# Two attention mixers of the second block: other places for the projections and for the result blocks among the heads' steps

## The reference

```python
h = rms_norm_2(x, norm_mix[l]) * (1 + sc_a) + sh_a
proj = h @ w_in[l]                                    # 1024 -> 3072 features
mq, mk, mv, dq, dk, dv = jnp.split(proj, splits, axis=-1)     # six parts of 512
mq = apply_partial_rope(rms_norm_2(heads(mq, MOBA_HEADS, HEAD_DIM), moba_q_norm[l]), cos, sin)   # mk, dq, dk alike
o_m = rms_norm_2(moba_attention(mq, mk, mv), moba_out_norm[l])          # 8 heads of 64
o_d = rms_norm_2(diff_attention(dq, dk, dv, lam), diff_subln[l]) * (1.0 - lam_init)   # 4 heads, two score matrices each
x = x + g_a * (jnp.concatenate([o_m, o_d], axis=-1) @ w_out[l])
```

## Time and profile before

| | us |
|---|---|
| median of three runs | 2174.84 (2174.81 to 2177.36) |
| the profiled execution | 2174.54 |
| its span on the engines | 2172.7 |
| layer 0's mixer, first product to last product's end (PE) | 1431.98 to 1601.53 |
| layer 1's mixer | 1811.94 to 1970.07 |

### The profile page before, as it was taken

One profiled execution on the slowest core, in us unless ns is written; L12 is line 12 of the kernel. 1 busy time (PEld: TensorE's weight loads), 2 busy tenths in 40 slices (PEclk: granted clock), 3 DMA queues, 4 the chain that ended last, 5 costly groups with the idle time before them and its releaser, 6 DMA issues.

```text
span 2172.7 us, 28353 instructions
## 1 busy us (share of the span) xinstructions
PE 1996.6 (92%) x11530; PEld 1728.1 (80%) x11530; DVE 1680.0 (77%) x1765; ACT 1174.4 (54%) x1318; POOL 72.8 (3%) x121
## 2 busy tenths in 40 slices
PE   6878999978889999999999999877889999889999
PEld 6666898777568888888788788667779999878998
DVE  6675888877588889899899988888668896846444
ACT  3443333364367776777777677545543445644432
POOL 6001000000100000000000000000010000000000
PEclk7988999998899999999999999978789999968999
DMA  9743799732389999999999999936229995313552
GB/s 350 240 168 136 281 335 366 277 129 97 137 303 330 350 367 355 338 354 371 337 344 363 368 333 352 320 115 223 70 98 345 349 370 163 131 48 128 180 189 97
DMA packets 251209, 554.37 MB, mean 255 GB/s; under 512 B 10077, under 2 KB 75857, under 8 KB 251073
## 3 DMA queue, kind: packets, MB, share of 16 engines
q1 hardware_dynamic: 247252, 544.13, 70.3%
q0 software_dynamic: 3552, 8.29, 1.2%
q10 hardware_dynamic: 268, 0.07, 0.0%
HBM read 551.40 MB, written 1.05 MB: 254 GB/s over the span
## 4 chain that ended last, share of the span: by engine, by line
PE 71%; DVE 14%; ACT 7%; DMA 4%; issue 4%; SPq 0%; ACTq 0%; DVEq 0%
PE bank L497 21%; PE bank L498 21%; PE bank L499 21%; DVE ring_lo L1914 4%; ACT ring_hi L1239 3%; DMA ring<-in_w_in_dram 2%; PE bank L886 1%; DVE acc L1854 1%; DMA ring<-in_ffn_w_dram 1%; PE bank L579 1%; DMA ring<-in_ada_w_dram 1%; PE bank L1064 1%; PE bank L548 1%; DVE XN L2158 1%; DVE work L2096 1%
## 5 line engine op out<-in xcount | busy, mean ns | idle before, releaser
L1914 DVE TENSOR_TENSOR ring_lo<-ring,ring_hi 128x2048 fp32r<-128x2048 f32 x417 | 949.9, 2285 | 267.7 <-ACT ring_hi L1239 265.1
L1239 ACT ACTIVATE ring_hi<-ring 128x2048 fp32r<-128x2048 f32 x417 | 795.5, 1913 | 493.0 <-PE bank L499 239.2
L497 PE MATMUL bank<-hh,ring_hi 128*128 128x256 f32 x1152 | 333.1, 289 | 19.9 <-ACT QK L1433 8.8
L498 PE MATMUL bank<-hl,ring_hi 128*128 128x256 f32 x1152 | 331.0, 287 | 0.0
L499 PE MATMUL bank<-hh,ring_lo 128*128 128x256 f32 x1152 | 330.6, 287 | 0.0
L497 PE MATMUL bank<-ring_hi,hh 128*128 128x256 f32 (+2 forms) x672 | 217.8, 324 | 39.4 <-ACT PT L1383 10.2
L497 PEld LDWEIGHTS bank<-hh,ring_hi 128*128 128x128 f32 x1152 | 226.4, 197 | 24.7 <-issue 14.1
L499 PE MATMUL bank<-ring_hi,hl 128*128 128x256 f32 (+2 forms) x768 | 241.9, 315 | 0.0
L497 PE MATMUL bank<-ring_hi,hgh 128*128 128x512 f32 (+1 forms) x576 | 220.3, 383 | 8.9 <-DVE ring_lo L1914 4.0
L498 PEld LDWEIGHTS bank<-hl,ring_hi 128*128 128x128 f32 x1152 | 226.5, 197 | 0.7 <-issue 0.2
L499 PEld LDWEIGHTS bank<-hh,ring_lo 128*128 128x128 f32 x1152 | 226.3, 196 | 0.0
(11 more groups left out here) (422 smaller groups left out, 2806.1 us busy)
## 6 DMA issues: line engine op xcount, KB each, us to landing
ring<-in_moe_w_dram SPq DMA_DIRECT2D x264, 1024.0 KB, 5.3
ring<-in_ada_w_dram SPq DMA_DIRECT2D x48, 1024.0 KB, 7.2
ring<-in_w_mod_dram SPq DMA_DIRECT2D x48, 1024.0 KB, 7.3
ring<-in_w_in_dram SPq DMA_DIRECT2D x40, 1024.0 KB, 6.4
ring<-in_ffn_w_dram SPq DMA_DIRECT2D x33, 1024.0 KB, 5.7
ring<-in_w_gate_dram SPq DMA_DIRECT2D x22, 1024.0 KB, 5.0
ring<-in_w_up_dram SPq DMA_DIRECT2D x22, 1024.0 KB, 5.1
ring<-in_w_down_dram SPq DMA_DIRECT2D x22, 1024.0 KB, 5.0
```

The costliest lines, as they stand in the source:

```text
L497: pe.matmul(ps, xh, wh, start=first, stop=False)
L498: pe.matmul(ps, xh, wl, start=False, stop=False)
L1239: act.activation(ring_hi[i % NH][:, 0:z], ring[n % NS][:, 0:z], ACT.Copy).then_inc(*s.hi(("hi", home(s, i), i)))
L1914: dve.tensor_tensor(ring_lo[n % NS][:, 0:z], ring[n % NS][:, 0:z], hi, ALU.subtract).then_inc(*s.lo(("lo", home(s, i), i)))
```

## The change

- The list of blocks (`WIN2`) and all three programs take the projections 6, 7, 8, 9, 0, 1 first (before: 6 to 11). So two projections of values (10, 11) leave the front, and 2, 3, 10, 11, 4 lie among the differential heads' steps, 5 among the first steps of the block attention.
- On PE the projections 2, 3, 11, 4 and 5 are cut in two pieces by tile of tokens (24 matmuls each), with a step of the heads between the pieces (2 and 3 share a gap: second piece of 2, first of 3). Projection 10 stays whole.
- Result blocks 2 and 3 are cut in the same way (24 matmuls into 12 and 12): before, block 2 stood whole after step 4 of the block attention and block 3 whole behind all steps. Now they are put as pieces after steps 4, 5 and 7; the second piece of block 3 stands where the whole one stood.
- In `last_blocks` the first tile of tokens now takes all of block 0 before block 1.
- The projections take their banks from `R2`, no longer from `R`.
- ACT and DVE follow the new order. The split of result block 1 moves from behind all heads' work to step 7 (`out_block(3)` on ACT, `block("wout2", 3)` on DVE). The transposes' copies of group 2 come before group 3's squares; the sums of squares and the root of group 0 come ahead of the first head; some splits are ahead of the place of their projection (`halves_for`). A head waits only for the values' block that holds its own columns (`wv`).

The diff, without the lines of `out_block`'s and the heads' dictionaries that only carry the new arguments:

```diff
-        WIN2 = [6, 7, 8, 9, 10, 11, 0, 1, 2, 3, 4, 5]
+        WIN2 = [6, 7, 8, 9, 0, 1, 2, 3, 10, 11, 4, 5]
...
-                    for h in range(2):
-                        for i in blocks:
-                            if t == 0 and h == 0:
-                                pe.wait_ge(*at("y", name, l, i))
-                            wh, wl = weights(main, name, l, i)
-                            for k in range(2):
...
+                    for h, i in ([(h, i) for i in blocks for h in range(2)] if t == 0 else [(h, i) for h in range(2) for i in blocks]):
+                        if t == 0 and h == 0:
+                            pe.wait_ge(*at("y", name, l, i))
+                        wh, wl = weights(main, name, l, i)
...
-                def project(i):
-                    summed(turn_of["win2", l, i])
+                def project(i, tiles=range(2)):
+                    if 0 in tiles:
+                        summed(turn_of["win2", l, i])
+                        psum2(*M, "proj", i)
...
-                    ps = psum(*M, "proj", i)
-                    for t in range(2):
+                    ps = R2.of(*M, "proj", i)
+                    for t in tiles:
...
-                for i in (6, 7, 8, 9, 10):
+                R2.start()
+                for i in (6, 7, 8, 9):
                     project(i)
                 turn_group(2)
-                project(11)
+                project(0)
+                project(1)
                 turn_group(3)
                 diff = attention((*M, "diff"), diff_heads(l))
-                for i in range(4):
-                    next(diff)
-                    project(i)
+                moba = attention((*M, "moba"), moba_heads(l))
                 next(diff)
+                project(2, (0,))
+                next(diff)
+                project(2, (1,))
+                project(3, (0,))
+                next(diff)
+                project(3, (1,))
+                project(10)
                 turn_group(0)
-                project(4)
                 next(diff)
-                project(5)
+                project(11, (0,))
+                next(diff)
+                project(11, (1,))
+                next(diff)
+                project(4, (0,))
                 turn_group(1)
                 next(diff)
-                moba = attention((*M, "moba"), moba_heads(l))
-                next(moba)
-                next(moba)
+                project(4, (1,))
+                next(moba)
+                project(5, (0,))
+                next(moba)
+                project(5, (1,))
                 next(moba)
                 to_features((*M, "yT"), YK, [[(*M, "diff")]] * 2, range(2, 4))
                 next(moba)
                 next(moba)
-                out_block("wout2", l, 2, [], True)
-                for i in range(5, 11):
-                    next(moba)
+                out_block("wout2", l, 2, [("free", *key) for key in R2.held if key], True, (0,))
+                R2.start()
+                next(moba)
+                out_block("wout2", l, 2, [], True, (1,))
+                next(moba)
+                next(moba)
+                out_block("wout2", l, 3, [], False, (0,))
+                next(moba)
+                next(moba)
+                next(moba)
                 to_features((*M, "yT"), YK, [[(*M, "moba", 0)]] * 2, (0,))
-                out_block("wout2", l, 3, [], False)
+                out_block("wout2", l, 3, [], False, (1,))
                 to_features((*M, "yT"), YK, [[(*M, "moba", 1)]] * 2, (1,))
                 last_blocks("wout2", l, 0, 1)
 
...
-                         wv=[(*M, "v", j) for j in range(2)] if h == 0 else []) for h in range(8)]
+                         wv=[(*M, "v", h // 4)] if h % 4 == 0 else []) for h in range(8)]
...
-                         wv=[(*M, "v", j) for j in (2, 3)] if h == 0 else [], lam=lam[:, l:l + 1]) for h in range(4)]
+                         wv=[(*M, "v", 2 + h // 2)] if h % 2 == 0 else [], lam=lam[:, l:l + 1]) for h in range(4)]
...
-                    act.activation(dst, R.of(*M, "proj", i)[:, :].rearrange("p (t c) -> p t c", t=2), ACT.Copy).then_inc(
+                    act.activation(dst, R2.of(*M, "proj", i)[:, :].rearrange("p (t c) -> p t c", t=2), ACT.Copy).then_inc(
...
+                def halves_for(i):
+                    high_halves(main, ahead(turn_of["win2", l, i]))
...
+                turn_group(2)
                 squares(3)
                 sd((*M, "qk", 3), stat(16, *M, "qk", 3))
-                project(10, vt(2))
-                values_in(2)
-                turn_group(2)
-                project(11, vt(3))
-                values_in(3)
+                project(0, gb(0, 0), (*M, "group turned", 2, 1))
+                project(1, gb(0, 1))
                 turn_group(3)
+                squares(0)
+                sd((*M, "qk", 0), stat(16, *M, "qk", 0))
                 diff = attention((*M, "diff"), diff_heads(l), 0.125)
+                moba = attention((*M, "moba"), moba_heads(l), 0.125)
                 next(diff)
-                project(0, gb(0, 0), (*M, "group turned", 2, 1))
+                halves_for(2)
                 next(diff)
-                project(1, gb(0, 1))
-                squares(0)
-                next(diff)
-                sd((*M, "qk", 0), stat(16, *M, "qk", 0))
                 project(2, gb(1, 0), (*M, "group turned", 3, 1))
+                halves_for(3)
                 next(diff)
                 project(3, gb(1, 1))
                 squares(1)
+                project(10, vt(2))
+                values_in(2)
+                turn_group(0)
                 next(diff)
-                turn_group(0)
+                next(diff)
                 sd((*M, "qk", 1), stat(16, *M, "qk", 1))
-                project(4, vt(0))
-                values_in(0)
+                project(11, vt(3))
+                values_in(3)
                 next(diff)
-                project(5, vt(1))
-                values_in(1)
                 turn_group(1)
                 next(diff)
                 sd((*M, "diff"), stat(8, *M, "diff", "ss"))
-                moba = attention((*M, "moba"), moba_heads(l), 0.125)
-                next(moba)
-                next(moba)
-                next(moba)
+                project(4, vt(0))
+                values_in(0)
+                next(moba)
+                halves_for(5)
+                next(moba)
+                next(moba)
+                project(5, vt(1))
+                values_in(1)
                 mixed(M, range(2, 4), scale)
                 next(moba)
                 next(moba)
                 out_block(2)
-                for i in range(5, 9):
-                    next(moba)
+                next(moba)
+                next(moba)
+                next(moba)
+                out_block(3)
+                next(moba)
                 roots_next()
...
                 mixed(M, range(1, 2), scale)
-                out_block(3)
                 out_block(0)
                 out_block(1)
...
+                    variance(gi)
+
+                def variance(gi):
+                    ss = stat(16, *M, "qk", gi)
+                    settled()
+                    dve.tensor_scalar(ss, ss, 1.0 / 64, 1e-6, ALU.mult, ALU.add).then_inc(*vec((*M, "qk", gi, "var")))
 
                 def normed(gi):
                     ss = stat(16, *M, "qk", gi)
                     x4 = GB[:, gi % 2, :, :].rearrange("p t (h d) -> p t h d", h=8)
-                    rstd((*M, "qk", gi), ss, 64, 1e-6)
+                    dve.wait_ge(*at(*M, "qk", gi, "sd"))
+                    dve.reciprocal(ss, ss).then_inc(*vec())
...
+                turn_group(2)
                 sums_of_squares(3)
                 normed(3)
-                block("win2", 10)
-                turn_group(2)
-                block("win2", 11)
+                block("win2", 0)
+                block("win2", 1)
                 turn_group(3)
+                sums_of_squares(0)
                 diff = attention((*M, "diff"), diff_heads(l), 0.125)
+                moba = attention((*M, "moba"), moba_heads(l), 0.125)
                 next(diff)
-                block("win2", 0)
-                next(diff)
-                block("win2", 1)
-                sums_of_squares(0)
+                block("win2", 2)
                 next(diff)
                 normed(0)
-                block("win2", 2)
+                block("win2", 3)
                 next(diff)
-                block("win2", 3)
+                turn_group(0)
                 sums_of_squares(1)
                 next(diff)
-                turn_group(0)
+                block("win2", 10)
+                next(diff)
                 normed(1)
-                block("win2", 4)
+                block("win2", 11)
                 next(diff)
-                block("win2", 5)
                 turn_group(1)
                 next(diff)
                 diff_variance()
-                moba = attention((*M, "moba"), moba_heads(l), 0.125)
```

(11 more changed lines are left out.)

33 lines of the change are left out of this document (18 added, 15 removed).

## The result

The changed kernel takes 2162.37 us (median of 5 runs, 2158.98 to 2166.89), the kernel before in the same comparison 2176.53 (5 runs): ratio 0.9938, 95% interval 0.9924 to 0.9953, so 14 us faster. The forecast was 2159.7.

What follows compares the result with a forecast made beforehand. No engine full: steps pass between PE, DVE and ACT. Layer 0 -9.1 + 0.8 - 1.3 + 1 = -8.6, layer 1 -7.9 + 0.4 + 0.3 + 1 = -6.2; 2174.5 - 14.8 = 2159.7 us, range 2149 to 2170.

Steps and rivals of the forecast that it cites:

- (c): End of the mixer, from the transposes of the first four heads' results to the last product: -9.1 and -7.9 us.
- (b): Block attention, from head 4's scores to the transposes of the first four heads' results: +0.8 and +0.4 us.
- Rival 2: Matmuls put between the block attention's steps hide nowhere: +2.8 to +5.2 us a layer, 2166.7 us; chance 0.15.
- (a): Mixer's front and differential heads, up to head 4's scores: -1.3 us in layer 0, +0.3 in layer 1, before handovers.
- the six pieces' handovers: Cut pieces in each layer: some 0.1 us each for handing over and change of matmul kind, +1 us a layer.
- PE's gain is mostly taken back by DVE: Heads' part: DVE, busy 48.4 of 60 us, keeps its queue in nearly the old order, leaving -1.3 us in layer 0.
- rival 1: DVE does not hold the heads' part; PE's 3.4 us gain goes through in both layers: 2151.9 us; chance 0.13.
- The new waits: PE waits for the projections' copy (ACT into PT) before the values of heads 0 and 2, 1 to 4 us each.
- Rival 5: Values' copies and splits ahead of exponentials cost their whole 1.9 us at four places a layer: +15, 2174.9 us; chance 0.08.
- Table loads: ACT's loads in each mixer fall from six to four, 1.28 us each, beside PE's projections; counted as nothing.
- Rival 3: Cutting projections lets PE's clock fall, 2.4 us a piece, 29 us in all: 2188.5 us; chance 0.07.
- Rival 4: Feed-forward stage behind layer 0, DMA engines busy at 0.95, gives back layer 0's gain: 2168.3 us; chance 0.04.

Runs made afterwards that it cites:

- b3: Kernel before with only two parts of the change: block 0 ahead of block 1 for the first tile, result block 1's split at step 7; ratio 0.9976.
- a1: Changed kernel with result block 3 whole behind all steps, its first 12 matmuls no longer behind step 7; 2166.0 us, ratio 0.9951 to the kernel before.
- b2: Kernel before with only the split of result block 1 moved to step 7 on ACT and DVE, PE's instructions unmoved; ratio 0.9966.
- a6: a4 with result block 1's split a step earlier, table load, squares and DVE's sums ahead of turned heads 6 and 7; 2153.4 us, ratio 0.9882.
- a2: Changed kernel with result block 2 whole behind step 4, 24 matmuls there and none behind step 5; ratio 0.9934 to the kernel before.
- a3: Changed kernel with the new order kept but every projection between heads whole, none cut by tile; ratio 1.0008 to the kernel before.
- b kernels: Three versions of the kernel before, with the last blocks' new order only, the moved split only, or both; ratios 0.9978, 0.9966, 0.9976.
- a8: Changed kernel with the norm weights and rotation of groups 0 and 1 left out, 5.3 us less DVE work a layer; ratio 0.992 to the kernel before.
- a4: Changed kernel with ACT's copies of projections 10 and 11 (the values) ahead of their ring_hi; 2157.8 us, ratio 0.9909 to the kernel before.

## Why the prediction was right, and where it was not

**(c)**, forecast -9.1 and -7.9, measured -9.5 and -7.9. Its two parts are shown: no wait for the split (b3), and 12 matmuls gone from it (a1). The 48 last matmuls took 11.2 us (forecast 48 x 0.23), the 12 before them 4.6 (4.4).

**(b)**, forecast +0.8 and +0.4, measured +1.1 and -0.2. The 12 matmuls hide (a1), the moved split costs 2.2 us a layer (b2, forecast 1.9 + 0.4). The chain through ACT that the forecast added up is the one that binds: reordering it, with DVE's sums behind it, gave 2.3 us back (a6). What the forecast did not price apart is the cut of result block 2, worth 2.5 and 1.1 (a2). Rival 2 is ruled out.

**(a)**, forecast -0.3 and +1.3 with the handovers, measured -0.7 and +3.0. In layer 1, 1.1 of it is the front, which took 39.2 to 40.2 us in the nine other kernels with the same front, so that execution's own. The step that failed is the last one of (a), +1 us a layer for the six pieces' handovers: by a3 the cut is worth -8.4 and -8.6 us (-7.2 and -6.4 with the copy first), and it offsets a cost of about the same size that the forecast did not see either, 7.8 and 10.5 us (a3 against before), in which the waits for the values stand. Two terms of about 8 us were taken for two of about 1. What the change of banks gives was not tested apart: the 1.6 us for a bank are there in the b kernels, which keep the old banks, and gone in the changed one. That the forecast's (a) came out within 2 us a layer of the measured one, and the total with it, is luck in this part: the two missed terms have opposite signs. "PE's gain is mostly taken back by DVE" is true in layer 0 (a8: 4.1 of 5.3 us), and mostly not in layer 1, where rival 1's view fits better; rival 1's gain did not show since new waits stood in its place. The prediction's list of PE's waits also passes over those for combined weights, 3.2 and 2.4 us before, which are 4.0 and 4.7 now.

**The new waits** for the values' copy came where forecast, before heads 0 and 2: 3.2 and 0.2 us in layer 0, 1.2 and 2.2 in layer 1, where 1 to 4 was forecast for each. The 1.2 is listed under another releaser, as the first row here shows (PE of the changed kernel). But the tile's copy on ACT, in the second row, had begun 0.72 us before PE went on and DVE's `st` is nothing that this product reads:

```profile
1871.99 0.46 PE L714 MATMUL bank<-PT,work 128*128 128x128 f32 x2 [1.21 <-DVE st L2416]
```

```profile
1871.27 0.57 ACT L1577 ACTIVATE PT<-bank 128x512 f32<-128x512 f32 x1
```

Taking most of them away gave 2.3 and 1.6 us (a4). Rival 5, all four at full price, is out.

**Table loads** went from six to four in each mixer, as forecast, at 1.28 us each in both traces. What they gave was not measured alone.

**Rival 3** (the clock falls with the cuts) is refuted: 0.91 in 1480 to 1540, where before had 0.87, and in the same order 0.88 over layer 0's heads' part with cuts and 0.82 without. The page "TensorE: Matmul & The Clock Gate" of the Trainium skill (A second HAM failure mode: psum-queue depth-cycling) tells of a kernel whose frequent micro-idles between groups of matmuls made the clock swing between its two levels. Of the two kernels in the new order, the one with the longer idle times has the lower clock here, and that is the uncut one: PE is idle for 15.9 of 79.5 us there, for 11.6 of 71.1 in the cut one. **Rival 4**: the stage between the mixers kept its 210.3 us.

**The first block's mixers**, forecast nothing. The sum there went by 0.23 us a matmul. In the changed kernel's execution the clock was 0.72 over these first six microseconds, where before had 1.00, and with 18 matmuls ahead in place of 12 DVE now waits for PE:

```profile
189.54 0.50 PE L497 MATMUL bank<-ring_hi,hh 128*128 128x512 f32 x1 [2.10 <-DVE yl L2021]
...
195.56 0.69 DVE L2028 TENSOR_TENSOR XN<-bank,gate 128x512 f32<-128x512 f32 x1 [1.28 <-PE bank L499]
...
211.66 0.55 PE L497 MATMUL bank<-hh,ring_hi 128*128 128x256 f32 x1 [2.28 <-ACT hT L1316]
```

Before, the last of these rows was

```profile
212.97 0.55 PE L497 MATMUL bank<-hh,ring_hi 128*128 128x256 f32 x1 [2.28 <-ACT hT L1294]
```

so from the first of these products to the next stage's first it took 22.1 us and before 20.5. Of the twelve other kernels eleven have the new order for the first tile; six of them show this wait of 1.3 us and five do not (a8: 20.5 us). The start of layer 0's mixer moved by only 0.6 us all the same, less than it moves from run to run, so the times do not show this loss.

**The chances.** The closing line gives 0.07 for a time within 4.3 us of before and 0.08 for a slower one, but rival 5 (no change) had 0.08 and rival 3 (slower) 0.07: the two figures are interchanged.

## What to carry to other kernels

When an order is new and also cut finer, price both against the kernel with the order alone: here each was worth about 8 us a layer, or 4 to 7 once the values' copies stood first, with opposite signs. Before work is put between the steps of a chain, look at the in-order queue of each helper engine: a 0.6 us copy behind a 1.9 us split cost 1.6 to 2.3 us a layer (a4), another order of split, table load and copies was worth 2.3 us more (a6), and the twelve matmuls put between the steps cost nothing there (a1). Neither swap moved an instruction of PE. A stretch ends on one engine's queue; read in that queue what stands ahead of the last thing the others wait for.

## What the runs showed that was not expected

- In the new order the same matmuls ran at a granted clock of 0.88 and 0.94 over the heads' part in pieces of 24 between steps (0.90 in layer 1 in two other kernels), and at 0.82 and 0.86 in pieces of 48. In the old order pieces of 48 had 0.86 and 0.92.
- The granted clock also differs between executions of kernels with the same instructions on PE: result block 3's first 12 matmuls of 512 columns, behind the same step of layer 0, took 4.6 us in the changed kernel and 3.0 in a8, and the start of layer 0's mixer, behind 1430 us of the same program, varied by 13 us. A single execution tells a part of 2 us only by its waits, not by its length.
